# Even layer of a two-block transformer: gates and latent norms moved beside the input projection, and the latent up-projection loaded by parts with packed rotary rows

## The reference

```python
def even_mixer(x, w_in, mla_q_norm, w_uq, mla_kv_norm, w_ukv, ...):
    h = x @ w_in
    c_q, c_kv, k_pe, gq, gk, gv, g_lr, gr = _split(h, EVEN_SPLITS)   # 256,128,32,256,256,512,32,512
    q = (rms_norm(c_q, mla_q_norm) @ w_uq).reshape(b, s, 8, 64 + 32)
    q_pe = apply_rope(q[..., 64:], cos, sin)
    kv = (rms_norm(c_kv, mla_kv_norm) @ w_ukv).reshape(b, s, 8, 64 + 64)
    k_pe = apply_rope(k_pe, cos, sin)                  # one key part shared by 8 heads
    o_mla = mla_attention(q_nope, q_pe, k_nope, k_pe, v_mla)
    la_f = log_sigmoid(lr_f @ gate_w_fwd + gate_b_fwd) / 16          # la_b alike
    o_f = gla_chunked(gq * 64**-0.5, gk, gv, la_f)     # chunks of 64, o_b on flipped tokens
    o_gla = rms_norm(o_f + o_b, gla_norm) * silu(gr)
    return concatenate([o_mla, o_gla])
```

## Time and profile before

| what | value |
|---|---|
| median of 3 runs | 3581.34 us (3579.44 to 3584.34) |
| the profiled execution | 3584.01 us, its span 3582.2 us |
| PE busy | 3276.1 us (91%) |
| PEld / DVE / ACT / POOL busy | 2213.6 (62%) / 1306.7 (36%) / 959.3 (27%) / 274.5 us (8%) |
| DMA | 590.04 MB, mean 165 GB/s |

### The profile page before, as it was taken

One profiled execution on the slowest core, in us unless ns is written; L12 is line 12 of the kernel. 1 busy time (PEld: TensorE's weight loads), 2 busy tenths in 40 slices (PEclk: granted clock), 3 DMA queues, 4 the chain that ended last, 5 costly groups with the idle time before them and its releaser, 6 DMA issues. The chain is left out here.

```text
span 3582.2 us, 40808 instructions
## 1 busy us (share of the span) xinstructions
PE 3276.1 (91%) x16378; PEld 2213.6 (62%) x16378; DVE 1306.7 (36%) x1781; ACT 959.3 (27%) x1576; POOL 274.5 (8%) x391
## 2 busy tenths in 40 slices
PE   7999999999999999999956889999997998999996
PEld 5885578887886577888744367444435557544442
DVE  3415554343523555343444553111115656111112
ACT  3325433232323524232231432000003453100001
POOL 1004200000102400000000410000000221000000
PEclk9999999999999999999977999999998999999998
DMA  5310132322430023222200123999993211799996
GB/s 149 117 48 25 60 94 94 94 94 57 130 113 24 1 94 106 94 94 80 85 7 15 47 84 136 422 424 424 424 414 99 72 47 55 290 420 424 424 424 279
DMA packets 232339, 590.04 MB, mean 165 GB/s; under 512 B 36582, under 2 KB 148148, under 8 KB 183036
## 3 DMA queue, kind: packets, MB, share of 16 engines
q1 hardware_dynamic: 232188, 587.92, 43.5%
HBM read 581.59 MB, written 2.10 MB: 163 GB/s over the span
## 5 line engine op out<-in xcount | busy, mean ns | idle before, releaser
L2377 PE MATMUL ps<-w_ring,xe 128*64 128x512 f32 x1024 | 234.4, 600 | 5.8 <-PEq L119 5.1
L330 PE MATMUL ps<-h_hi,in_w_hi 128*128 128x512 f32 (+1 forms) x528 | 209.9, 398 | 13.7 <-DVE in_w_lo L386 7.9
L386 DVE TENSOR_TENSOR mlp_w_lo<-w_ring,mlp_w_hi 128x2048 fp32r<-128x2048 f32 x62 | 142.1, 2292 | 212.8 <-ACT mlp_w_hi L351 212.8
L330 PE MATMUL ps<-h_lo,in_w_hi 128*128 128x512 f32 (+1 forms) x528 | 208.3, 394 | 0.0
L330 PE MATMUL ps<-h_hi,in_w_lo 128*128 128x512 f32 (+1 forms) x528 | 208.0, 394 | 0.0
L330 PE MATMUL ps<-h_hi,mlp_w_hi 128*128 128x512 f32 x512 | 202.6, 396 | 1.9 <-DVE h_lo L394 1.9
L330 PE MATMUL ps<-h_hi,mlp_w_lo 128*128 128x512 f32 x512 | 202.5, 396 | 0.0
L330 PE MATMUL ps<-h_lo,mlp_w_hi 128*128 128x512 f32 x512 | 202.5, 395 | 0.0
L330 PE MATMUL ps<-mlp_w_hi,u_lo 128*128 128x512 f32 x512 | 202.3, 395 | 0.0
L330 PE MATMUL ps<-mlp_w_lo,u_hi 128*128 128x512 f32 x512 | 202.2, 395 | 0.0
L330 PE MATMUL ps<-mlp_w_hi,u_hi 128*128 128x512 f32 x512 | 202.2, 395 | 0.0
(11 more groups left out here) (538 smaller groups left out, 6672.8 us busy)
## 6 DMA issues: line engine op xcount, KB each, us to landing
w_ring<-in_w SPq DMA_DIRECT2D x192, 1024.0 KB, 12.6
ex_front<-in_w SPq DMA_DIRECT2D x96, 1024.0 KB, 13.1
ex_back<-in_w SPq DMA_DIRECT2D x96, 1024.0 KB, 13.4
w_ring<-in_w_in SPq DMA_DIRECT2D x32, 1024.0 KB, 6.0
w_ring<-in_w_up SPq DMA_DIRECT2D x32, 1024.0 KB, 5.5
w_ring<-in_w_down SPq DMA_DIRECT2D x32, 1024.0 KB, 5.0
w_ring<-in_cmp_w SPq DMA_DIRECT2D x16, 512.0 KB, 4.8
w_ring<-in_w_out SPq DMA_DIRECT2D x8, 1024.0 KB, 6.0
```

The costliest lines, as they stand in the source:

```text
L330: mm = pe.matmul(ps[0:o.rows, bank[k], 0:o.cols], lhsT, rhs, start=(o.first and j == 0), stop=(o.final and j == len(o.mm) - 1))
L386: dve.tensor_tensor(w.lo[:, n % SPLITS, 0:used], ring.slots[:, n % RING, 0:used], w.hi[:, n % SPLITS, 0:used].bitcast(F32), ALU.subtract). ...
L2377: mm = pe.matmul(ps[rows, bank + half, :], lhsT, slot(2 * m + a)[:, kk, 512 * half:512 * half + 512], start=(k == 0), stop=(k == DC - 1))
```

## The change

The stages `gg`, `ge`, `gf`, `mn`, `cs`, `re` and `kp` are gone. `even_beside` puts the work of the first five (the same instructions apart from buffers, and no separate cosine on POOL) into `ei` as side work, and `ei` cycles over 4 PSUM banks instead of 8, the other 4 being for the side work. POOL clears each ring slot in `ei` after its last tile is split, instead of all at the head of `gs`. `gs` waits for the mask tables only after the state chain, and its SP prefetches the up-projection weights once its outputs are done. These weights are loaded as six DMAs that gather the 32 rotary columns of the eight heads into two groups of 128 and the other columns behind them, and likewise keys and values of `w_ukv`. `uq` then has 14 outputs: 2 of packed rotary query rows, 4 of query pairs, 4 of key pairs, 4 of values, over 5 banks, with the rotary turn as side work on packed rows.

```diff
+def even_beside(nc, ctx, ps, C, I, x, ring, n_split, cq, ckv, cs, gq, gk, lr, og, gains, add, back):
...
+    def sums_and_gates(pe, s):
+        pe.wait_ge(s.e_tables, landed)
+        for n in range(3):
+            pe.wait_ge(s.e_squared, n + 1)
+            pe.matmul(ps[0:2, SUM_BANK, :], add[:, n, :], squares[n], start=(n == 0), stop=(n == 2)).then_inc(s.e_summed, 1)
+        pe.wait_ge(s.evac_v, s.done_v[3])
+        for n in range(3):
+            pe.matmul(ps[:, SUM_BANK + 1 + n, :], gw[:, n % 2, n // 2 * P:(n // 2 + 1) * P], lr[:, :], start=True, stop=True).then_inc(s.e_z, 1)
...
+    def exponentials(*ns):
+        def go(act, s):
+            if ns[0] == 0:
+                decays(act, s)
+            for n in ns:
+                c, d = jobs[n]
+                act.wait_ge(s.e_left, n + 1)
...
+                if n >= 2:
+                    act.wait_ge(s.e_mixed, n - 1)
+                act.activation(ex[n % 2][:, 0, :], cum[:, at(c, d), :], ACT.Exp).then_inc(s.e_exped, 1)
...
+    def mix(*ns):
+        def go(dve, s):
+            for n in ns:
+                c, d = jobs[n]
+                dve.wait_ge(s.e_exped, 3 * n + 3)
...
+    def pool(pool, s):
+        for n in range(LAST - RING + 1, LAST + 1):
+            pool.wait_ge(s.split, n_split(n))
+            pool.memset(ring.slots[:, n % RING, :], 0.0)
...
+    side = beside(names, sp,
+                  {5: sums_and_gates, 7: last_gate, 8: spread, 21: flip(0, 1), 23: flip(2, 3)},
+                  {3: square_queries, 4: square_keys, 6: roots_and_gates, 7: sigmoids, 10: round_chunks, 15: exponentials(0, 1), 17: exponentials(2, 3),
+                   22: keep_a(0), 24: keep_a(2)},
+                  {2: final_norm(0), 3: final_norm(1), 4: final_norm(2), 5: final_norm(3), 7: inverses, 9: scale, 10: logs, 11: scans,
+                   13: totals, 14: then(rest_of_chunks, left_over), 16: mix(0), 17: mix(1), 19: mix(2), 20: mix(3),
+                   22: keep_v(1), 24: keep_v(3)},
+                  pool, {3: load_tables})
...
@@ gla, stage gs @@
+                sp.wait_ge(s.out_done, TT)
+                ring.prefetch(sp, nxt)
-                pool.memset(ring.slots[:, :, :], 0.0).then_inc(s.zeroed, 1)
                 pool.memset(att[:, :, :, :], 0.0).then_inc(s.zeroed, 1)
-                dve.wait_ge(s.zeroed, 2)
-                dve.wait_ge(s.small_in, 16 * 9)
...
+                dve.wait_ge(s.zeroed, 1)
+                dve.wait_ge(s.small_in, 16 * 9)
...
@@ mla_tiles, load @@
+            for k in range(kc):
+                src, c = w[k * P:(k + 1) * P, :].rearrange("p (h e) -> p h e", h=8), 0
+                for a, b in order:
+                    moves.append((slot[:, k, c:c + 8 * (b - a)].rearrange("p (h e) -> p h e", h=8), src[:, :, a:b]))
...
+    return [tile(2, 768, by_part(w_uq, 2, ((HD, 96), (0, HD))), queries),
+            tile(1, 1024, by_part(w_ukv, 1, ((0, HD), (HD, P))), keys_and_values)]
...
@@ ropes_beside @@
+    def turn_queries(g):
+        def go(dve, s):
+            dve.wait_ge(s.t_swapped, 2 + g)
+            dve.tensor_tensor(tmp[:, g, :], ps[:, TURN_BANK + g, :], sin[:, :], ALU.mult).then_inc(s.t_parts, 1)
+            dve.tensor_tensor(turned[:, g, :], turned[:, g, :], cos[:, :], ALU.mult).then_inc(s.t_parts, 1)
+            dve.wait_ge(s.t_parts, 4 + 2 * g)
+            for a in range(4):
+                rows = slice(32 * a, 32 * a + 32)
+                dve.tensor_tensor(qh[rope_rows, 4 * g + a, :], turned[rows, g, :], tmp[rows, g, :], ALU.add)
...
+    return beside("t_swapped t_parts t_key", lambda sp, s: None, {0: swap_key, 3: swap_queries(0), 4: swap_queries(1)},
+                  {n: copy_keys(m) for n, m in ((4, 0), (6, 2), (8, 4), (10, 6))}, {0: turn_key, 6: turn_queries(0), 8: turn_queries(1)}, nothing)
```

More of the change, by code:

```diff
@@ L847, in _ @@
                         take(step - LAG)
[L850 to L883, removed]
-                        dve.wait_ge(s.cosined, n)
-                        dve.wait_ge(s.sined, n)
-                        dve.tensor_tensor(x, x, tmp[0:r, (n - 1) % 4, 0:w], ALU.add).then_inc(s.added, 1)
 def log_sigmoid(act, dve_ready, act_chain, z, t):
@@ L1760, in even_mixer @@
-            tiles = [tile(2, 768, lambda slot: [(slot, W(w_uq, 2, 0, 768))],
-                          lambda w: [fm(w, cs, 96 * j, 96, range(2), **to(qh[:, j, :], "AV"[j % 2], sc)) for j in range(8)]),
-                     tile(1, 1024, lambda slot: [(slot, W(w_ukv, 1, 0, 1024))],
-                          lambda w: [fm(w, cs[:, 2:3, :], 128 * j, HD, range(1), **to(kh[0:HD, j, :], "AV"[j % 2])) for j in range(8)]
-                          + [out(P, 512, products(cs[:, 2, i * P:(i + 1) * P], Pair(*(part[:, 0, :].rearrange("p (h e) -> p h e", h=8)[:, :, HD:P]
-                                                                                       for part in (w.hi, w.lo)))),
-                                 **to(vm[:, i, :], "AV"[i % 2])) for i in range(TT)])]
@@ L1767, in even_mixer @@
-            sums_norm(nc, "mn", ps, C, [(cq[:, 0, :], gains[:, 0:1]), (cq[:, 1, :], gains[:, 1:2]), (ckv[:, 0, :], gains[:, 2:3])],
-                      add, back[:, :, :], ring, tiles)
-            split_into(nc, "cs", [(cq[:, j, :] if j < 2 else ckv[:, 0, :], cs[:, j, :], None) for j in range(3)])
-            gemm(nc, "uq", ps, ring, tiles, RING)
-            rope(nc, "re", ps, [(c, cos, sin) for c in [qh[:, j, :] for j in range(8)] + [kx[:, :]]], perm)
-            with stage(nc, "kp", "copied") as (block, s):
-                @block.vector
-                def _(dve):
-                    for j in range(0, 8, 2):
-                        dve.tensor_copy(kh[64:96, j, :], kx[64:96, :])
-                @block.scalar
-                def _(act):
-                    for j in range(1, 8, 2):
-                        act.activation(kh[64:96, j, :], kx[64:96, :], ACT.Copy)
+            turned = sb("turned", [P, 2, T], c2)
@@ L1782, in even_mixer @@
+            w_cs += [qh, kh, vm, turned]
+            gemm(nc, "uq", ps, ring, uq, RING, side=ropes_beside(nc, c2, ps, qh, kh, kx, turned, perm, cos, sin), banks=TURN_BANK)
         groups = [Names(chunk=c, qk=lambda a, c=c: (qh[:, 2 * c + a, :], kh[:, 2 * c + a, :]),
@@ L2588, in constants @@
     c["c_sin1"] = np.where((q % 64 < 8)[:, None], -c["c_sin1"], c["c_sin1"])
-    for n, rot, rows, starts, size in ((2, 32, [16] * 64 + list(range(16)) * 2, (64,), 96), (3, 64, list(range(32)) * 4, (0, 64), P)):
+    for n, rot, rows, starts, size in ((2, 32, list(range(16)) * 8, (0, 32, 64, 96), P), (3, 64, list(range(32)) * 4, (0, 64), P)):
         ax = rot // 2
```

330 lines of the change are left out of this document (238 added, 92 removed).

## The result

| | time, us | ratio to before, 95% interval |
|---|---|---|
| before, same chip | 3582.84 (3579.44 to 3584.49, 4 runs) | |
| the changed kernel | 3498.38 (3493.59 to 3500.95, 4 runs) | 0.9764 [0.9747, 0.9781] |

The change gains 84.5 us (2.4%); 3507 was forecast, with a range of 3497 to 3524. The profiled execution took 3498.67 us, its span 3496.9 us.

What follows compares the result with a forecast made beforehand. PE bounds `ei`; the stages after it are hand-over chains with barriers. -42.7 + 13.7 + 1.0 - 7.2 - 18.8 - 20.4 = -74.4 us from 3584.0 gives 3509.6; the median lies 2.7 lower: 3507 us, range 3497 to 3524.

Steps and rivals of the forecast that it cites:

- rival 5: More is gained: fast matmuls from the start of `uq`, fast clock in `gs`, no wait before output 20: 3499 us; chance 0.08.
- `gg`, `ge`, `gf`, `mn`, `cs` removed: These stages disappear between `ei` and the attention: -42.7 us for the first three, -18.8 us for the last two.
- PE's side work in `ei`: Seven fp32 matmuls (6.2 us), sixteen transposes (1.8) and six narrow matmuls (1.4) lie on PE's path in `ei`: 9.4 us.
- 3.1 us of waiting: In `ei`, PE finishes output 19 at 1815.0 us and waits for the last tile until 1818.0 before output 20.
- 0.5 us more: In `ei` after output 20's wait, for `mix` products, copies of outputs 17 and 19 and transposes that follow closely.
- Memsets, 1.0 us: POOL's slot clearing in `ei` slows DVE beside it: 1 us taken, between nothing and 2.2 us.
- Tail, 0.7 us: At the end of `ei`, DVE has one kept transpose behind its last copy: 0.7 us.
- `gs`, -7.2 us: Without the memset, DVE's state chain starts 1.3 us into `gs` instead of 8.50 us: -7.2 us.
- `uq`, `re`, `kp`, -20.4 us: The three stages become one, 45.6 us to 25.2 us, its end set by DVE after output 7.
- The six loads, 0: The gathered up-projection weight loads, 6144 short runs, land within 11.7 us of cover: nothing lost, 1.5 us at most.
- Rival 2: PE's clock falls in `ei`, 2.6 us each fall: 3509.6 us, or 3529 if down from output 16; chance 0.06.
- my own sign of error: The prediction called itself wrong if, among other signs, anything outside the changed stages moved by over 3 us.

Runs made afterwards that it cites:

- e7: The changed kernel with DVE's four differences in `ei` moved ahead of the lo parts of the latents: 3497.74 us, ratio 0.9757.
- e4: The changed kernel with the ring's memset again at the head of `gs` instead of in `ei`: 3503.23 us, ratio 0.978.
- e2: The changed kernel with the old up-projection, rotary turn and key copies (three stages, 84 matmuls) put back: 3525.83 us.
- e11: The kernel of e2 once more, unaltered (the changed kernel with the old up-projection, turn and key copies): 3524.5 us.
- e3: The kernel before with only the new up-projection (loads by part, packed turn): 3559.61 us, ratio 0.9932.
- e6: The changed kernel with the second rotary turn of the queries in `uq` one output earlier: 3499.06 us, ratio 0.977.
- e8: The changed kernel with 42 extra, unread fp32 matmuls of 256 columns on PE in the tail of `gs`: 3507.17 us, ratio 0.979.
- e12: The kernel before, unaltered, timed and traced a second time: 3583.32 us.
- e9: The changed kernel with the edits of e6 and e7 and 22 extra, unread matmuls in the tail of `gs`: 3502.92 us.
- e1: The changed kernel once more, unaltered: 3499.65 us, ratio 0.9764.

## Why the prediction was right, and where it was not

In the windows of the earlier trace rows the stretch from `ei` to the attention was to shrink by 74.4 us and shrank by 78.4: 275.0 to 196.6, where the prediction's sign was 200 to 202. The medians fell by 84.5, so 4.0 of the 10.1 us beyond the forecast lie in the stretch and 6.1 outside, where nothing was forecast. The median came 8.6 us below 3507, just outside the 8 us that had the chance of 0.70. It lies in the range because the lower end was set by rival 5, whose reasons are mostly not those of the gain; that part of the hit is luck. The mechanism, removed stages against side work that PE pays for, is borne out term by term.

1. **`gg`, `ge`, `gf`, `mn`, `cs` removed, -42.7 and -18.8:** right, they are gone from the trace.
2. **PE's side work in `ei`, 9.4 us:** 9.9 measured. Besides, each return to the projection's matmuls costs 0.1 us (0.34 between two starts instead of 0.235, 0.22 instead of 0.12), five times: 10.4.
3. **"3.1 us of waiting" before output 20, and "0.5 us more":** this is the step that failed: the trace shows 0.1 us in place of the 3.1. Counted from the stage's first rounding (1722.79 before, 1720.72 after), the walk had the first difference at 86.1 us (1808.9); the chip had it at 86.0. From there the walk took "1.5 us for table and decays", 3.4 us of exponentials, then both parts of the tile, up to 95.2 us (1818.0). The table load did not lie behind the difference, so decays and exponentials took 3.3 us (1806.74 to 1810.00), and the lo part ended at 93.5 (1814.2). PE was to finish output 19 at 92.2 (1815.0) and finished it at 93.5 as well, by the side work and the returns of point 2 and a head slower by 0.3. The wait was a difference of two sums of over 90 us: 1.7 us off on one side and 1.3 on the other made all of it. e7 moved one side by 1.9 us and gained at most 0.5. Of the "0.5 us more" some 0.3 came, inside the 9.9 of point 2: the first eight transposes followed the products closely and took 1.33 instead of 1.04 us.
4. **Memsets, 1.0 us:** nothing. My nearest row was a POOL instruction that reads, and the 1 us was a choice between it and nothing. The Trainium skill (SBUF — State Buffer, "Who interferes with whom") says that a write-only GpSimd instruction does not hold up such DVE work; by it the term was 0, and e4 and the 0.69 us rows agree.
5. **Tail, 0.7 us:** 0.6. The stage's head added 0.3: the slower transposes, which DVE mostly hid (its wait fell from 2.38 to 1.03 us). `ei` grew by 12.0 us in all (0.6 more than I can assign), where 13.7 + 1.0 = 14.7 were forecast.
6. **`gs`, -7.2 us:** -7.6, the chain starting at 1.3 us as said. e4 gave 6.8 of it back with the memset alone; the rest was not taken apart.
7. **`uq`, `re`, `kp`, -20.4 us:** -21.3 (24.3 us against 25.2). e2, e11 and e3 put 20.4 to 20.7 us on this half. Output 7 was copied 15.8 us into the stage and not at 17.4, and DVE's list behind it took 8.3 us and not 7.8. "The first 13 go at 0.435 us" was too many: the slow time is about as long as before (5.3 and 5.7 us), but in the new stage the key's swap (1.99 us) uses up a part of it, and matmuls are at the fast rate from 1898.4. The walk to "16.0 us" also holds a third swap that its words leave out; with two it comes to 15.2. That DVE's chain behind output 7 sets the end was right: e6 took out what it said.
8. **The six loads, 0:** right. What a load costs here is its issue on SP within the stage's barrier, a term that the prediction doesn't have; 4.7 us of it fitted into the stage.
9. **Rival 2, the clock in `ei`:** it didn't come, but my argument against it was bad. I took one execution's head of `ei` (3.56 us of waiting, then clock 1.00) as what a wait does. In thirteen of fourteen traces the clock was down for most of the transposes behind that wait. Had there been 3.1 us of waiting before output 20, one row was no ground to call a fall unlikely. The Trainium skill (TensorE: Matmul & The Clock Gate, "Part 1") says that the array returns to 1.2 GHz after an idle stretch; it does not say so of any gap, and my sentence left that condition out. Thirteen traces agree with it at this wait of 3.55 us, the first one doesn't.

10. **Rival 5, "3499 us":** the time that came, by other sums. Its two prices make 5.7 us and 3501; the last 2 us stand for a fast clock in `gs` without a price, and `gs` was only 0.4 us shorter than summed. Its missing wait is true; its fast matmuls at the start of `uq` are not, and e8 shows that they would have been worth 1.5 to 1.8 us, not 2.6. Most of the way from 3507 is the 6 us outside the stretch.

**Outside the stretch** the median fell by another 6 us, against a forecast of nothing, and "if anything outside these stages moves by over 3 us" was my own sign of error: 4.1 us moved "behind", 4.8 from the first exponential to the end. The sign was too narrow, since one and the same kernel moves by 5.2 and 5.0 us (e12). Ahead of `ei`, the kernels lie together (1714.9 to 1724.4). Behind, the three executions with the old gates took 1133.1 to 1138.2 us, the eleven others 1127.7 to 1137.4, ten of them under 1133.1; to the very end the three took 1579.4 to 1584.4, the ten 1572.7 to 1577.7 and e9 1582.4. Two parts of unchanged code make most of this: from the first row of `ye_hi` in the even layer to the first rounding of the last mixer's weights (448.3 to 448.9 against 445.0 to 447.2, e9 449.1), and from there to the first exponential of the last attention (92.3 to 93.8 against 88.4 to 90.2, e1 93.1, e9 93.6). So perhaps 3 us of the gain come from work that was not touched. No run here says why, and it stays open; so does why e2's timed runs stand 26 us above the changed kernel's when its trace shows 20.8.

## What to carry to other kernels

When work of idle engines is put beside a stage that PE bounds, price what PE itself must issue, with a tenth of a microsecond for each switch, and trust that part; a wait forecast as the difference of two walked engines is known only to a few microseconds, so keep it in the range and out of the sum. Don't read a rule about the clock from one execution: the same wait had a fast clock behind it once and a slow one thirteen times. And where stages end in a barrier, count DMA issues on the issuing queue as work of the stage, by number and not by bytes: here 0.71 to 0.80 us for each gathered load of 32 to 256 KB.
